# A two-layer hybrid encoder on one core: weight splits at stage ends, 512-column token units, alternating score parts, high products first

## What is computed

```
h = rms_norm(x, norm_pre); h = (silu(h @ w_gate) * (h @ w_up)) @ w_down
x = x + 0.5 * rms_norm(h, norm_post)                 # FFN, hidden width 2816
proj = rms_norm(x, mix_norm_pre) @ w_in              # mixer
y = concat(rglru(...), window_attention(...), diff_attention(...)) @ w_out
x = x + rms_norm(y, mix_norm_post)
```

## Time and profile before

| | |
|---|---|
| median of 3 runs | 1001.85 us (1000.99 to 1002.21) |
| profiled execution, its own time | 1003.56 us |
| its span | 1001.8 us |
| PE busy | 971.3 us, 97% |
| DVE busy | 665.4 us, 66% |
| ACT busy | 524.5 us, 52% |
| mean granted PE clock | 0.996 |
| HBM read | 178.92 MB, 181 GB/s over the span |

### The profile page before, as it was taken

One profiled execution on the slowest core, in us unless ns is written; L12 is line 12 of the kernel. 1 busy time (PEld: TensorE's weight loads), 2 busy tenths in 40 slices (PEclk: granted clock), 3 DMA queues, 4 the chain that ended last, 5 costly groups with the idle time before them and its releaser, 6 DMA issues.

```text
span 1001.8 us, 13665 instructions
## 1 busy us (share of the span) xinstructions
PE 971.3 (97%) x5638; PEld 848.4 (85%) x5638; DVE 665.4 (66%) x869; ACT 524.5 (52%) x695; POOL 25.1 (3%) x44
## 2 busy tenths in 40 slices
PE   6999999999999999999999999999999999999997
PEld 5888888889987888888888888887999888888886
DVE  4865765676887765656677675656778777565654
ACT  3653544557764653535555444545576555544442
POOL 0130000000001200000000000000000000000000
PEclk8999999999999999999999999999999999999999
DMA  8588565537434665565447655655553346656551
GB/s 277 169 242 303 171 198 180 168 127 252 129 125 127 189 231 189 186 193 181 156 148 247 197 197 179 197 182 174 184 179 112 111 142 215 197 182 195 183 168 43
DMA packets 131469, 180.87 MB, mean 181 GB/s; under 512 B 4064, under 2 KB 114792, under 8 KB 131408
## 3 DMA queue, kind: packets, MB, share of 16 engines
q1 hardware_dynamic: 129216, 176.24, 53.6%
q0 software_dynamic: 2192, 3.76, 1.9%
HBM read 178.92 MB, written 2.63 MB: 181 GB/s over the span
## 4 chain that ended last, share of the span: by engine, by line
PE 84%; DVE 7%; DMA 3%; ACT 3%; issue 2%; SPq 0%; DVEq 0%; ACTq 0%
PE UP L406 29%; PE Y L428 20%; PE UP L408 14%; PE UP L647 9%; PE Y L462 2%; DMA raw<-in_ffn_w_up 2%; PE Y L418 2%; DVE wlo L1021 2%; PE Y L456 1%; DVE x L1080 1%; DMA raw<-in_ffn_w_gate 1%; PE Y L457 1%; PE Y L568 1%; DVE xs L1075 1%; PE UP L436 1%
## 5 line engine op out<-in xcount | busy, mean ns | idle before, releaser
L1021 DVE TENSOR_TENSOR wlo<-raw,whi 128x2048 fp32r<-128x2048 f32 x159 | 363.7, 2291 | 151.2 <-ACT whi L733 150.8
L406 PE MATMUL UP<-xT,whi 128*128 128x512 f32 x1280 | 453.9, 399 | 0.9 <-DVE gate L1160 0.9
L733 ACT ACTIVATE whi<-raw 128x2048 fp32r<-128x2048 f32 x159 | 304.1, 1912 | 106.6 <-DMA raw<-in_ffn_w_gate 77.8
L408 PE MATMUL UP<-xT,wlo 128*128 128x256 f32 x1280 | 359.3, 281 | 0.0
L406 PEld LDWEIGHTS UP<-xT,whi 128*128 128x128 f32 x1280 | 240.6, 188 | 60.6 <-DVE gate L1160 1.7
L408 PEld LDWEIGHTS UP<-xT,wlo 128*128 128x128 f32 x1280 | 242.0, 189 | 1.2
L428 PE MATMUL Y<-whi,yT 128*128 128x512 f32 x736 | 207.0, 392 | 1.1 <-DVE sm L1244 1.1
L428 PEld LDWEIGHTS Y<-whi,yT 128*128 128x128 f32 x736 | 135.1, 188 | 29.4 <-DVE sm L1244 1.5
L428 PE MATMUL Y<-wlo,yT 128*128 128x512 f32 x368 | 114.3, 392 | 0.0
L819 ACT ACTIVATE gate_small<-UP 128x512 f32<-128x512 f32 x40 | 23.8, 594 | 117.5 <-PE UP L408 117.5
L428 PEld LDWEIGHTS Y<-wlo,yT 128*128 128x128 f32 x368 | 69.1, 188 | 15.6
(11 more groups left out here) (184 smaller groups left out, 821.7 us busy)
## 6 DMA issues: line engine op xcount, KB each, us to landing
raw<-in_ffn_w_up SPq DMA_DIRECT2D x44, 1024.0 KB, 5.3
raw<-in_ffn_w_down SPq DMA_DIRECT2D x44, 1024.0 KB, 5.0
raw<-in_ffn_w_gate SPq DMA_DIRECT2D x43, 1024.0 KB, 5.3
raw<-in_w_in SPq DMA_DIRECT2D x20, 1024.0 KB, 5.3
raw<-in_w_out SPq DMA_DIRECT2D x8, 1024.0 KB, 4.9
gains<-in_ffn_norm_pre SPq DMA_DIRECT2D x4, 512.0 KB, 5.9
gains<-in_ffn_norm_post SPq DMA_DIRECT2D x4, 512.0 KB, 5.8
shift_scratch<-shift_rows POOLq DMA_DIRECT2D x1, 1536.0 KB, 13.9
```

The source lines that it names most:

```text
L406: nc.tensor.matmul(dst[:, 0:2 * S], h[:, kt, c:c + P], xT[:, kt, :, :].rearrange("p h s -> p (h s)"), start=kt == 0, stop=False, skip_grou ...
L408: mm = nc.tensor.matmul(dst[:, S:2 * S], o[:, kt, c:c + P], xT[:, kt, 0, :], start=False, stop=kt == KT - 1, skip_group_check=True)
L733: A.activation(whi[:, k % RING, :], raw[:, k % RING, :], ACT.Copy).then_inc(hi_ready, 1)
L1021: V.tensor_tensor(wlo[:, k % RING, :], raw[:, k % RING, :], whi[:, k % RING, :].bitcast(F32), ALU.subtract).then_inc(lo_ready, 1)
```

## The change

- `feature_tile` makes its eight products of 512 columns first, then the eight of 256 columns; the waits for high and low weights stand ahead of each run.
- `token_pair` replaces `token_units` in stages 1 to 5: both units are the moving operand of one product of 512 columns, high weights first, then low ones, then the low half of `xT`. The two units share a bank of `Y`, are released together, and the readers (`token_tanh`, `token_hidden`, `values_copy`) follow.
- The last unit's last bank is made in two pieces (`half_rows`, three products each) with the first turn of the next stage between them, also at the mixer's end. ACT squares bank 2 before it copies the first turned quarter, and bank 3 (with its root) before the second.
- The split of the next stage's unit 1 stands at the end of an FFN. In the mixer DVE's `sp(12)` comes behind the SWA weights and `job_lo(JOB_B)`, `sp(14)` ahead of `job_lo(JOB_SWA)`.
- `scores` alternates the parts, and makes all products of 256 columns before those of 128.
- OUT_A's first token half waits for one level of the SWA logits, the second for both.
- DVE's small parameters are cut in three, behind pairs 3, 4 and 5.

```diff
@@ -402,9 +402,12 @@
...
             def feature_tile(dst, k, c):
                 h, o = cols(k, whi), cols(k, wlo)
+                pe.wait_ge(hi_ready, k + 1)
                 for kt in range(KT):
                     nc.tensor.matmul(dst[:, 0:2 * S], h[:, kt, c:c + P], xT[:, kt, :, :].rearrange("p h s -> p (h s)"),
                                      start=kt == 0, stop=False, skip_group_check=True)
+                pe.wait_ge(lo_ready, k + 1)
+                for kt in range(KT):
                     mm = nc.tensor.matmul(dst[:, S:2 * S], o[:, kt, c:c + P], xT[:, kt, 0, :],
                                           start=False, stop=kt == KT - 1, skip_group_check=True)
                 return mm
@@ -419,6 +422,14 @@
...
+            def half_rows(k, parts, n):
+
+                h, o = rows(k, whi), rows(k, wlo)
+                act_hi, act_lo = parts[n]
+                for stat, mov, stop in ((act_hi, h, False), (act_hi, o, False), (act_lo, h, n == 1)):
+                    mm = nc.tensor.matmul(bank(Y, 3), stat[:, P:2 * P], mov[:, n, 512:1024], start=False, stop=stop)
+                return mm
+
...
@@ -436,6 +447,31 @@
...
+
+            def token_pair(s, t, first_signal):
+
+                k = stage_unit(s, 0)
+                assert k % RING + 1 < RING
+                tok, dst = slice(t * P, t * P + P), bank(Y, 2 * t).rearrange("p (u n) -> p u n", u=2)
+
+                def both(w, kt):
+                    return w[:, k % RING:k % RING + 2, UC * kt:UC * kt + UC]
+
+                if t == 0:
+                    pe.wait_ge(hi_ready, k + 2)
+                for kt in range(KT):
+                    if kt % 4 == 0:
+                        pe.wait_ge(xT_hi, quarter(s, t, kt // 4) + 1)
+                    nc.tensor.matmul(dst, xT[:, kt, 0, tok], both(whi, kt), start=kt == 0, stop=False)
+                if t == 0:
+                    pe.wait_ge(lo_ready, k + 2)
+                for kt in range(KT):
+                    nc.tensor.matmul(dst, xT[:, kt, 0, tok], both(wlo, kt), start=False, stop=False)
+                for kt in range(KT):
+                    if kt % 4 == 0:
+                        pe.wait_ge(xT_lo, quarter(s, t, kt // 4) + 1)
+                    mm = nc.tensor.matmul(dst, xT[:, kt, 1, tok], both(whi, kt), start=False, stop=kt == KT - 1)
+                mm.then_inc(unit_used if t else first_signal, 2)
...
@@ -452,22 +488,22 @@
...
-                        dst = bank(Y, 2 * t + n, 0, UC)
...
+                        dst = bank(Y, 2 * t, UC * n, UC * n + UC)
+                        nc.tensor.matmul(dst, xT[:, kt, 0, tok], cols(k, whi)[:, kt, :], start=kt == n == 0, stop=False, skip_group_check=True)
+                        nc.tensor.matmul(dst, xT[:, kt, 0, tok], cols(k, wlo)[:, kt, :], start=False, stop=False, skip_group_check=True)
...
-                token_units(s, 0, first_signal)
+                (token_pair if s else token_units)(s, 0, first_signal)
...
@@ -493,7 +529,6 @@
...
                     feature_tile(bank(UP, 0), k, 0)
                     feature_tile(bank(UP, 1), k, P).then_inc(unit_used, 1)
 
@@ -544,28 +578,36 @@
...
                         token_rows(k, hidden_parts(i), 1, 0, False, True).then_inc(y_banks, 1)
+                        half_rows(k, hidden_parts(i), 0)
                         if s + 1 < STAGES:
                             turn(s + 1, 0, 0)
-                        token_rows(k, hidden_parts(i), 1, 1, False, True).then_inc(unit_used, 1)
+                        half_rows(k, hidden_parts(i), 1).then_inc(unit_used, 1)
...
                 for n in range(4):
-                    part, r = n // 2, n % 2
-                    if j == JOB_SWA:
-                        q, k = swq[:, r, :], swk[:, r, :]
-                    else:
-                        head = r + (2 if j == JOB_B else 0)
-                        q, k = dqk[:, head, :], dqk[:, 4 + head, :]
+                    r, part = n // 2, n % 2
+                    q, k = operands(r, part)
                     half = slice(HD * part, HD * part + HD)
                     nc.tensor.matmul(SCORE_BANKS[part][:, S * r:S * r + S], q[half, P:S], k[half, :], start=True, stop=True)
+                for n in range(4):
+                    r, part = n // 2, n % 2
+                    q, k = operands(r, part)
+                    half = slice(HD * part, HD * part + HD)
                     mm = nc.tensor.matmul(SCORE_BANKS[2 + part][:, P * r:P * r + P], q[half, 0:P], k[half, 0:P],
                                           start=True, stop=True)
                 mm.then_inc(scores_done, 1)
@@ -688,9 +730,10 @@
...
-                pe.wait_ge(logits_ready, 2 * (l * JOBS + JOB_SWA) + 2)
+                pe.wait_ge(logits_ready, 2 * (l * JOBS + JOB_SWA) + 1)
                 out_ready(OUT_A, 1)
                 both_banks(out_unit(OUT_A), mixed(OUT_A), 0, True)
+                pe.wait_ge(logits_ready, 2 * (l * JOBS + JOB_SWA) + 2)
                 both_banks(out_unit(OUT_A), mixed(OUT_A), 1, True).then_inc(unit_used, 1)
...
@@ -707,8 +750,9 @@
...
+                half_rows(out_unit(OUT_SWA), mixed(OUT_SWA), 0)
                 turn(s + 1, 0, 0)
+                half_rows(out_unit(OUT_SWA), mixed(OUT_SWA), 1).then_inc(unit_used, 1)
 
             pe.wait_ge(ident_loaded, 16)
...
@@ -770,25 +814,24 @@
...
                 for t in range(NT):
                     if s:
                         square_y(s, t, 0)
                         if t:
-                            turned_hi(s, 0, 1)
+                            turned_hi(s, 0, 0)
                         square_y(s, t, 1)
                         norm_root(s, t, POST)
-                        if t == 0:
-                            for k in splits:
-                                split(k)
+                        if t:
+                            turned_hi(s, 0, 1)
                     for h in range(2):
                         square_x(s, t, h)
...
                     for h in range(2):
-                        if not (s and t == 0 and h == 1):
+                        if t or s == 0:
                             turned_hi(s, t, h)
...
@@ -805,9 +848,9 @@
...
                     if t == 0:
-                        act.wait_ge(tok_first, 2 * f + 1)
+                        act.wait_ge(tok_first, 2 * f + 2)
...
-                        act.wait_ge(unit_used, ffn_unit(s, "gate", 0) + 1)
+                        act.wait_ge(unit_used, ffn_unit(s, "up", 0) + 1)
...
@@ -847,17 +890,18 @@
...
+                split(last_unit(s) + 2)
                 load_root_table()
...
+                    A.activation(dv[:, t, :], bank(Y, 2 * t), ACT.Copy).then_inc(values_copied, 1)
...
@@ -1188,10 +1224,11 @@
...
-                    if s % 3 == 0 and i == 3:
-                        small_parameters(s // 3)
...
+                    if s % 3 == 0 and i in (3, 4, 5):
+                        small_parameters[i - 3](s // 3)
+                split(last_unit(s) + 2)
...
@@ -1351,23 +1396,23 @@
...
                 softmax_logits(JOB_SWA)
                 job_output(JOB_B)
-                sp(12)
                 softmax_weights(JOB_SWA)
                 gelu_cube()
                 job_lo(JOB_B, 2)
+                sp(12)
                 sp(13)
                 gelu_gate()
                 job_output(JOB_SWA)
                 output_lo(3, 0, lru_out[:, :, :])
+                sp(14)
                 job_lo(JOB_SWA, 4)
-                sp(14)
                 sp(15)
...
```

More of the change, by code:

```diff
@@ L461, in token_units @@
                             pe.wait_ge(xT_lo, quarter(s, t, kt // 4) + 1)
-                        mm = nc.tensor.matmul(bank(Y, 2 * t + n, 0, UC), xT[:, kt, 1, tok], cols(k, whi)[:, kt, :],
-                                              start=False, stop=kt == KT - 1)
+                        mm = nc.tensor.matmul(bank(Y, 2 * t, UC * n, UC * n + UC), xT[:, kt, 1, tok], cols(k, whi)[:, kt, :],
+                                              start=False, stop=n == 1 and kt == KT - 1, skip_group_check=True)
                     mm.then_inc(unit_used if t else first_signal, 1)
@@ L771, in load_root_table, with enter @@
                 A.activation(nw[:, 3, 3:4], epsb[:, :], ACT.Sqrt)
-            def enter(s, splits):
+            def enter(s):
                 for t in range(NT):
@@ L939, in mixer @@
                 sp(2)
-                values_copy(0, 0)
-                values_copy(1, 0)
+                values_copy(0)
                 sp(3)
-                values_copy(0, 1)
-                values_copy(1, 1)
+                values_copy(1)
                 sp(4)
@@ L999, in _ @@
             for s in range(STAGES):
-                enter(s, [stage_unit(s, 1)] if s and s % 3 != 2 else [])
+                enter(s)
                 if s % 3 == 1:
@@ L1138, in token_hidden @@
                     link(V.scalar_tensor_tensor(gate[:, t, :], tanh[:, t, :], 1.0, bank(Y, 2 * t, 0, UC), ALU.add, ALU.mult))
-                    if t == 0:
-                        dve.wait_ge(tok_first, 2 * f + 2)
```

(10 more changed lines are left out.)

25 lines of the change are left out of this document (13 added, 12 removed).

## The result

The changed kernel takes 979.07 us (median of 4 runs, 977.76 to 980.22) against 1002.03 us for the kernel before in the same rounds: ratio 0.9772, 95% interval 0.9755 to 0.9789. That is 23.0 us less, where 16.5 were forecast; the forecast was 985.3, the range 976 to 993. The profiled execution took 977.76 us, its span 976.0, at a granted clock of 0.997.

What follows compares the result with a forecast made beforehand. The prediction took the kernel as bound by PE's issue of matmuls plus some ten short stalls. Its terms summed to -16.5 us, 987.06 from the profiled 1003.56, or 985.3 against the median; range 976 to 993.

Steps and rivals of the forecast that it cites:

- part 1: FFN feature tiles, 512-column products first, then 256-column ones: -2.0 us over 160 tiles, bounds 0 and -8.4.
- part 4: Inside the two mixers, alternating score parts and later DVE splits: -3.0 us a mixer, -6.0 in all, bounds -1.4 and -3.7.
- Rival A: Feature tiles: order within a tile is worth its full bound, -8.4 in place of -2.0, giving 978.9 us; chance 0.25.
- Part 2: Token tiles of stages 1 to 5, two units joined as 512 columns: -0.25 us a tile, -1.2 for the second tiles.
- The +0.5 for the late load: Joined units release together, so an FFN's unit 5 load starts 0.97 us later: +0.5 us, bounds 0 and +1.5.
- Part 3: End of an FFN, stages 0, 2, 3: split moved out, `xs` earlier, PE's 1.09 idle gone; -1.65 us each, -5.0.
- Rival B: FFN ends: the late table load keeps the turn waiting, PE stalls about 2.6 us each, giving 993.1; chance 0.12.
- rival F: FFN ends: the table load has a 1.28 us tail, PE stalls 1.0 three times, giving 988.3; chance 0.04.
- Parts 4 and 5: Inside the mixers, -3.0 us each, -6.0; and at their ends, `xs` and second turn earlier, -1.1 each, -2.2.
- Part 6: Small parameters spread over three pairs: the longer `gate_sum` wait, in stage 0, goes; -0.6 us.
- Rivals C, D and E: Same-half-bank runs slower, 1023.7, chance 0.04; no scores overlap, 987.3, 0.05; joining saves next to nothing, 989.2, 0.05.

## Why the prediction was right, and where it was off

The time fell by 23.0 where 16.5 were forecast, in the range and on its lower side. Most of the mechanisms came as told; the two terms that were sized too small are the tiles (part 1) and the inside of the mixers (part 4). Step by step, by the distances above:

- **Part 1, the tiles: the step that failed in size.** Forecast -2.0; undoing it costs 6.4, doing it alone gives 6.9. The mechanism and both bounds stood. The count used 1.87 for a run of 512s, read behind an alternating tile in the earlier trace rows; behind a run of 256s it is 1.84. With 1.84, 0.955 and 5.47, all read from the new pair, the same formula gives 1.81 + 3 x 1.84 + 4 x 0.955 + 5.47 = 16.62, where the count had 16.76. Those 0.14, over 40 pairs, are 5.6 us. Rival A, with -8.4, was much nearer than the forecast, and its 978.9 almost meets the measured 979.07; that meeting is partly luck, for the tiles gave 1.5 to 2 less than its -8.4 and the mixers more than their forecast. Two slips in the text of this part change nothing: one tile in four, not in six, stands behind the down products, as its formula has it, and 160 x 0.054 is 8.6, the 8.4 being the pair's.
- **Part 2, the joined units: right.** 0.31 a token tile for 0.25, the second tile of stage 1 now 213.10 to 218.65. The isolated gap of the Trainium skill's page "TensorE: Matmul & The Clock Gate", section "Back-to-back issue gap", would have given 0.06, an estimate from that page's N/2.4 + 2.5 ns; the trace rules it out. The +0.5 for the late load did not occur in the changed kernel's profile and does in others. That stage 2 lost its wait of 0.3 for `gate_sum` instead was luck in part: of the eleven runs that vary the changed kernel seven have the wait.
- **Part 3, the FFN ends: right.** Stage 3 fell by 3.65; 1.77 of it is the tiles, 1.88 is left for entry and second token tile, where 1.65 + 0.25 stood: the second turn comes 1.12 sooner (1.18 forecast), the stretch to the next turns takes 7.76 for 8.17 (0.45), the rest 0.36 less (0.25). The chain was as worked out:

```profile
192.17 1.92 ACT L777 ACTIVATE whi<-raw 128x2048 fp32r<-128x2048 f32 x1 [2.14 <-DMA raw<-in_w_in]
194.10 1.28 ACT L815 ACT_TABLE_LOAD   x1
195.40 0.20 ACT L815 ACTIVATE nw<-epsb 128x1 f32<-128x1 f32 x1
195.50 0.58 ACT L786 ACTIVATE junk<-Y 128x512 f32<-128x512 f32 x1
```

```profile
202.91 0.60 PE L447 MATMUL UP<-ident,xs 128*128 128x128 f32 x4
...
204.40 1.17 PE L465 MATMUL Y<-whi,xT 128*128 128x512 f32 x4
205.80 1.19 PE L465 MATMUL Y<-whi,xT 128*128 128x512 f32 x4 [0.23 <-ACT xT L809]
```

  The late table pushes the first square, the turn waits for nothing, and the second quarter costs 1.40 instead of 0.9 to 1.0: the stall of 0.4. What the prediction does not name is that its 8.18 of before held a stall too, the 0.40 for the low copy (0.77 at the mixers' ends). By the rows the same reordering that makes the new stall takes the old one away: ACT squares bank 3 at 0.20 behind the second turn (204.25), where it was 1.13 (210.73), so DVE adds to `x` and makes the low copy sooner. No run undoes that order. Rival B did not come, and no tail stands behind the table load (0.02 us to the next instruction, so rival F is out: the drain of 1.38 us in the Trainium skill's page "ScalarE: Activation LUTs", section "What ACT_TABLE_LOAD costs", is not seen here).
- **Parts 4 and 5, the mixers.** -5.02 and -5.03 for -4.35 each (3.0 + 1.1 + 0.25). Up to the product behind the SWA turns, 69.65 from the landmark before and 65.88 now, a mixer gained 3.77 for 3.0; from there to the turns of token half 1 it gained 0.89 for 1.1; the second token tile gives the last 0.36. The scores were the step that was too small: 0.45 a block was taken, and for two blocks only, since the sum followed DVE's chain behind A and B; 0.75 came, in three, the full half that the Trainium skill's page "TensorE: Matmul & The Clock Gate", section "The mechanism", lets expect for products on different row groups. I had held the 128-column products for bound by their weight loads; they overlap too. The DVE order gave 1.7 for the 2.0 counted. The stall of 0.54 for the second level of the logits is gone, as forecast; no run undoes that edit. At the mixers' ends a stall of 1.4 stands where the prediction's own numbers give 1.47 (it turns at 315.04, and PE, free at 314.25 and without the three products moved behind the turn, arrives at 313.57). The two pieces that were part of this step gain nothing there: 0.15 is lost by them.
- **Part 6.** Stage 0 fell 0.8 more than stage 3; 0.6 were forecast. No run undoes this edit.
- Rivals C, D and E are refuted by the pair of 16.62, the block of 1.51 and the 0.31 a tile.

The medians say 23.0 less, the spans 25.8. The profiled execution of the kernel before lies 1.5 above its median and that of the changed kernel 1.3 below; 1.9 of these 2.8 are the start, which varies by more than that between runs.

How far the cause is shown: undone one at a time, the order in the tile costs 7.1 us by the distances and the split in the entry about 1.6 (both without stage 2's wait for `gate_sum`), the scores 4.2, the DVE split 3.5 and the joined units 3.3; the turn at the mixers' ends gains 0.3 when it is undone. That is some 19 of the 23.9 that the stretches behind the start gained. The other 4 to 5 belong to what no run undoes: the pieces and ACT's order at the FFN ends, the wait for one level of the logits, the small parameters, and the lucky load in stage 2.

## What to carry to other kernels

In a stream that is bound by matmul issue, look at the distance of two starts for each neighbourhood, not for each shape: the alternation of 512 and 256 columns cost 6.4 to 6.9 us over 160 tiles, 0.04 a tile, and any order with runs of at least two avoided most of it. Price a run by rows that have the same neighbours on both sides, or keep both bounds in the forecast. Count a saving in PE's own stream once for each place where it stands, not only along the chain that you follow. And when a boundary gets shorter, test whether its fillers are still needed (here 1.3 us an entry), and watch the first loads behind it.

## What the runs showed that was not expected

- Alternating 512- and 256-column products take 0.240 + 0.113 us, runs of two 0.465 + 0.232, runs of eight 1.84 + 0.955: per tile 2.82, 2.785 and 2.79, with 2.80 for runs of four between. Behind 256s the first five 512s of a long run take 0.232 each and the rest 0.227. The price by length of run is not monotone, and no run here says why.
- fp32 products on 64 partitions each overlap by pairs down to 128 columns when neighbours use different halves: eight products in 1.51 us for 2.26.
- Distances between landmarks on PE repeat within 0.1 us over executions whose total differs by more than 2 us; what varies is the first 31 to 33 us and single loads (the one in stage 2 took 6.2 to 8.1 us to land).
